# First feed-forward of a diffusion layer: tokens split 512 and 256, context high and low parts in one matmul

## What is computed

```python
def swiglu(h, w_gate, w_up, w_down):
    return (jax.nn.silu(h @ w_gate) * (h @ w_up)) @ w_down

def ffn_sublayer(t, shift, scale, gate, norm_g, w_gate, w_up, w_down):
    h = modulate(rms_norm(t, norm_g), shift, scale)
    return t + gate * (MACARON_WEIGHT * swiglu(h, w_gate, w_up, w_down))

x = ffn_sublayer(x, ml[0], ml[1], ml[2], ffn1_norm[i], ...)      # 512 tokens
ctx = ffn_sublayer(ctx, mc[0], mc[1], mc[2], ffn1_norm[i], ...)  # 256 tokens
```

## Time and profile before

| | |
|---|---|
| median of three runs | 1355.15 us (1355.12 to 1356.28) |
| span of the profiled execution | 1354.2 us |
| TensorE busy | 1333.5 us, 98% |
| VectorE busy | 865.3 us, 64% |
| ScalarE busy | 400.0 us, 30% |
| GpSimd busy | 651.0 us, 48% |

### The profile page before, as it was taken

The page is one execution under the profiler, slowest core; times in us unless marked ns, Lnnn a source line. Parts: engine busy times, 40 slices in busy tenths (PEclk is TensorE's granted clock), DMA queues, the critical chain, the costliest instruction groups (busy, mean ns, idle before and its releaser), DMA issues.

```text
span 1354.2 us, 21460 instructions
## 1 busy us (share of the span) xinstructions
PE 1333.5 (98%) x8546; PEld 1229.7 (91%) x8546; DVE 865.3 (64%) x1376; ACT 400.0 (30%) x757; POOL 651.0 (48%) x408
## 2 busy tenths in 40 slices
PE   5999999999999999999999999999999999999998
PEld 4899999999999999998888888888998999999997
DVE  5787368568556555437656649826778765555666
ACT  4320010210210110124635321222142555544455
POOL 1544444543543533532732356636467455655554
PEclk9999999999999999999999999999999999999999
DMA  9553354353444344223322479484736233344322
GB/s 357 161 148 85 121 148 120 120 157 116 126 135 139 102 126 158 62 55 109 80 62 52 126 212 259 152 266 148 229 87 199 63 94 94 107 115 114 101 72 85
DMA packets 236782, 178.18 MB, mean 132 GB/s; under 512 B 33416, under 2 KB 211852, under 8 KB 236684
## 3 DMA queue, kind: packets, MB, share of 16 engines
q1 hardware_dynamic: 216624, 145.78, 37.6%
q10 hardware_dynamic: 20060, 31.04, 7.0%
HBM read 156.93 MB, written 19.86 MB: 131 GB/s over the span
## 4 chain that ended last, share of the span: by engine, by line
PE 93%; DVE 3%; DMA 2%; SPq 1%; issue 1%; ACT 0%; DVEq 0%; ACTq 0%
PE ps L1244 47%; PE ps L1971 13%; PE ps L1566 13%; PE ps L2030 7%; DMA ada_w<-in_ada_w_dram 2%; PE ps L1255 1%; PE ps L1844 1%; DVE ada_acc L2860 1%; DVE ps L2972 1%; PE ps L2057 1%; PE ps L1881 1%; PE ps L1669 1%; PE ps L1487 1%; PE ps L1438 1%; PE ps L1706 1%
## 5 line engine op out<-in xcount | busy, mean ns | idle before, releaser
L1143 POOL TENSOR_SCALAR w_hi<-w_raw 128x1024 fp32r<-128x1024 f32 x128 | 153.4, 1198 | 527.8 <-PE ps L1244 276.0
L1146 POOL TENSOR_TENSOR w_lo<-w_raw,w_hi 128x1024 fp32r<-128x1024 f32 x128 | 325.4, 2542 | 10.7
L1244 PE MATMUL ps<-h_hi,w_lo 128*128 128x384 f32 (+2 forms) x1000 | 291.4, 351 | 0.0
L1244 PE MATMUL ps<-h_hi,w_hi 128*128 128x384 f32 (+2 forms) x1000 | 287.1, 346 | 0.0
L1244 PE MATMUL ps<-h_lo,w_hi 128*128 128x384 f32 (+2 forms) x1000 | 287.0, 346 | 0.0
L1244 PEld LDWEIGHTS ps<-h_hi,w_lo 128*128 128x128 f32 x1000 | 178.8, 188 | 14.9 <-issue 4.3
L1244 PEld LDWEIGHTS ps<-h_lo,w_hi 128*128 128x128 f32 x1000 | 180.6, 188 | 10.5
L1244 PEld LDWEIGHTS ps<-h_hi,w_hi 128*128 128x128 f32 x1000 | 180.4, 188 | 10.7
L1222 POOL TENSOR_TENSOR w_lo<-w_raw,w_hi 128x512 fp32r<-128x512 f32 x90 | 115.6, 1297 | 105.7 <-ACT w_hi L2609 104.2
L2860 DVE SCALAR_TENSOR_TENSOR ada_acc<-ada_w,cs,ada_acc 128x1024 f32<-128x1024 f32 x70 | 108.3, 1581 | 7.8 <-DMA ada_w<-in_ada_w_dram 5.5
L1971 PE MATMUL ps<-h_hi,w_hi 128*128 128x256 f32 x360 | 102.0, 283 | 0.0
(11 more groups left out here) (459 smaller groups left out, 2635.0 us busy)
## 6 DMA issues: line engine op xcount, KB each, us to landing
w_raw<-in_ffn_w_gate_dram SPq DMA_DIRECT2D x44, 512.0 KB, 5.1
w_raw<-in_ffn_w_up_dram SPq DMA_DIRECT2D x44, 512.0 KB, 4.1
w_raw<-in_ffn_w_down_dram SPq DMA_DIRECT2D x44, 512.0 KB, 4.5
ada_w<-in_ada_w_dram ACTq DMA_DIRECT2D x32, 512.0 KB, 3.9
w_raw<-in_w_in_dram SPq DMA_DIRECT2D x32, 512.0 KB, 4.3
ada_w<-in_ada_w_dram SPq DMA_DIRECT2D x30, 512.0 KB, 4.3
c_scr<-cp ACTq DMA_DIRECT2D x16, 288.0 KB, 3.8
b_scr<-bt_sb ACTq DMA_DIRECT2D x16, 256.0 KB, 3.9
```

The source lines that it names most:

```text
L1143: pool.tensor_scalar(w_hi[:, s, 0:cols], w_raw[:, s, 0:cols], 1.0, 1.0, ALU.mult, ALU.mult)\
L1146: pool.tensor_tensor(w_lo[:, s, 0:cols], w_raw[:, s, 0:cols], w_hi[:, s, 0:cols].bitcast(F32), ALU.subtract).then_inc(w_split, 1)
L1244: last = pe.matmul(mv[2], st, mv[part], start=(first and q == 0), stop=(n == len(terms) - 1 and q == 2))
```

## The change

The tokens of a gate, up or down job are now split 512 (latents) and 256 (context). The latents fill the first bank. The second bank holds two halves of 256: the high weights meet the context's high and low parts in a single matmul of 512 columns, whose moving operand has two pieces (h_pair, act_pair: the same places as before, allocated as one tile), and the low weights meet the high part in one of 256 columns that adds into the first half. A k-step has five matmuls instead of six. VectorE adds the two halves by a reduction of [128, 256, 2] to half_sum in SBUF, once behind the gate job and once behind the up job. ScalarE's silu is split in two, the second part reading half_sum and waiting for gate_summed; only it frees the pair. The product is split in two, 512 and 256. The reduction of the gate job stands first in each tile's part of VectorE's loop. The down's three adds become 256, 512 and 256. The free columns are gone in both banks of a job, so the folded sums move to the bank of the side job (in the late segment to a pair that isn't in use yet). The sums of segment 0 stay at their place, in gate 3's second bank.

```diff
-    h_hi = place("h_hi", [P, KD, NT], F32R)
-    h_lo = place("h_lo", [P, KD, NT], F32R)
+    h_pair = place("h_pair", [P, 2, KD, NT], F32R)
+    h_hi, h_lo = h_pair[:, 0, :, :], h_pair[:, 1, :, :]
...
+    act_pair = place("act_pair", [P, 2, SEG, NT], F32R)
+    act_hi, act_lo = act_pair[:, 0, :, :], act_pair[:, 1, :, :]
...
+    half_sum = place("half_sum", [P, 2, NC], F32, at=fold_at + 4 * KB)
...
+    def ctx_half(j, part):
+        return ctx_(j)[:, NC * part:NC * part + NC]
...
     def ada_sum_cols(j):
-        return lat(j)[:, ADA_COL:ADA_COL + 2 * KD]
+        return ctx_(j)[:, ADA_COL:ADA_COL + 2 * KD]
...
+                if summed:
+                    last = folded_sums(ada_sum_cols(j), summed)
                 last.then_inc(job_done, 1)
...
+                    def pair_step(j, wh, wl, hi, lo, pair, first, final, between=None):
+                        def mm(q, o, st, mv, start, stop):
+                            ins = pe.matmul(o, st, mv, start=start, stop=stop)
+                            if between and q is not None:
+                                between(q)
+                            return ins
+                        mm(None, ctx_(j), wh, pair, first, False)
+                        mm(0, ctx_half(j, 0), wl, hi[:, NL:NT], False, final)
+                        mm(None, lat(j), wl, hi[:, 0:NL], first, False)
+                        mm(1, lat(j), wh, lo[:, 0:NL], False, False)
+                        return mm(2, lat(j), wh, hi[:, 0:NL], False, final)
...
-                            for q in range(2):
-                                pe.matmul((lat, ctx_)[q](js.gu(v))[:, 0:384], st[:, k, :],
-                                          h_hi[:, k, 384 * q:384 * q + 384], start=(k == 0 and r == 0), stop=False)
+                            for o, c in ((lat(js.gu(v)), slice(0, NL)), (ctx_half(js.gu(v), 0), slice(NL, NT))):
+                                pe.matmul(o, st[:, k, :], h_hi[:, k, c], start=(k == 0 and r == 0), stop=False)
...
+                        if two:
+                            last = pair_step(j, wh[:, k, c], wl[:, k, c], act_hi[:, k, :], act_lo[:, k, :], act_pair[:, :, k, NL:NT],
+                                             k == 0, k == tiles - 1)
...
                         if n == NT:
-                            dst, src = dst.rearrange("p (b c) -> p b c", b=2), both(jg, 384)
-                        act.wait_ge(job_done, (jg + 1) + i * part.jseg)
+                            act.activation(dst[:, 0:NL], src, ACT.Silu)
+                            act.wait_ge(gate_summed, i * SEG + (part.segs * SEG + f + 1))
+                            dst, src = dst[:, NL:NT], half_sum[:, 0, :]
                         act.activation(dst, src, ACT.Silu).then_inc(slot_read[jg % 4], 1)
...
                     for f_ in range(tiles):
                         jg, ju = js.gu(2 * f_), js.gu(2 * f_ + 1)
+                        if n == NT:
+                            done(jg)
+                            sum_halves(jg, 0).then_inc(gate_summed, 1)
                         if part.side:
...
+                            up = tokens(ju)
+                            link(sum_halves(ju, 1))
...
+                        elif n == NT:
+                            STT(up[:, 0:NL], up[:, 0:NL], 0.5, sl[:, 0:NL], ALU.mult, ALU.mult)
+                            STT(up[:, NL:NT], half_sum[:, 1, :], 0.5, sl[:, NL:NT], ALU.mult, ALU.mult).then_inc(gu_ok, 1)
...
+                            half = STT(x[:, k, c], ctx_half(j, 0), mod[:, g, 1:2], x[:, k, c], ALU.mult, ALU.add)
+                            own[0] += 1
+                            half.then_inc(dve_own, 1)
+                            STT(x[:, k, 0:NL], lat(j), mod[:, g, 0:1], x[:, k, 0:NL], ALU.mult, ALU.add)
+                            dve.wait_ge(dve_own, own[0])
+                            ins = STT(x[:, k, c], ctx_half(j, 1), mod[:, g, 1:2], x[:, k, c], ALU.mult, ALU.add)
...
+            def sum_halves(j, n):
+                return dve.tensor_reduce(half_sum[:, n, :], ctx_(j).rearrange("p (h c) -> p c h", h=2), AX.X, ALU.add)
```

More of the change, by code:

```diff
@@ L1330, in _, with s5_side @@
             keep_busy(5)
-            def s5_side(i, v, j):
+            def s5_side(i, v, j, summed):
                 h = v // 2
@@ L1479, in slot_free, with pair_job @@
                         pe.wait_ge(slot_read[j % 4], j // 4 + i * (part.jseg // 4))
+                    def pair_step(j, wh, wl, hi, lo, pair, first, final, between=None):
[9 more added lines that the diff above has]
+                        return mm(2, lat(j), wh, hi[:, 0:NL], False, final)
+                    def pair_job(j, wh, wl, between=None):
+                        for k in range(KD):
+                            last = pair_step(j, wh[:, k, :], wl[:, k, :], h_hi[:, k, :], h_lo[:, k, :], h_pair[:, :, k, NL:NT], k == 0, k == KD - 1,
+                                             (lambda r: between(k, r)) if between else None)
+                        return last
                     joint = 2 if two and part.segs + i == 0 else 0
@@ L1492, in joint_lo @@
                         wh = wv((u0 + v) % 4, KD, P)[0]
-                        for q in range(2):
-                            last = pe.matmul((lat, ctx_)[q](js.gu(v))[:, 0:384], wh[:, k, :],
-                                             h_lo[:, k, 384 * q:384 * q + 384], start=False, stop=(k == KD - 1))
+                        pe.matmul(lat(js.gu(v)), wh[:, k, :], h_lo[:, k, 0:NL], start=False, stop=(k == KD - 1))
+                        last = pe.matmul(ctx_half(js.gu(v), 1), wh[:, k, :], h_lo[:, k, NL:NT], start=False, stop=(k == KD - 1))
                         if k == KD - 1:
@@ L1540, in sums_between @@
                                     ada_sum(ada_ctx_cols(js.gu(v - 1)), ADA_START, n)
-                            last = split_mm(terms, sums_between)
+                            last = pair_job(j, wh, wl, sums_between)
+                        elif two:
+                            if part.late and v == 3:
+                                pe.wait_ge(tail_cols_read, 1)
+                            last = pair_job(j, wh, wl)
+                            if part.late and v == 1:
+                                slot_free(js.gu(3))
+                                last = folded_sums(ada_sum_cols(js.gu(3)), g)
                         else:
                             last = split_mm(terms)
-                        if two and nth and g and v == 1:
-                            last = folded_sums(ada_sum_cols(j), g)
                         if not two and nth == 0 and v == 2 * tiles - 1:
@@ L1563, in down_step @@
                         c = slice(P * q, P * q + P)
-                        for r, (st, mv) in enumerate(((wl, act_hi), (wh, act_lo), (wh, act_hi))):
-                            for bank, cols in down_banks(j, two):
-                                last = pe.matmul(bank, st[:, k, c], mv[:, k, cols], start=(k == 0 and r == 0),
+                        if two:
+                            last = pair_step(j, wh[:, k, c], wl[:, k, c], act_hi[:, k, :], act_lo[:, k, :], act_pair[:, :, k, NL:NT],
+                                             k == 0, k == tiles - 1)
+                        else:
+                            for r, (st, mv) in enumerate(((wl, act_hi), (wh, act_lo), (wh, act_hi))):
+                                last = pe.matmul(lat(j), st[:, k, c], mv[:, k, 0:NL], start=(k == 0 and r == 0),
                                                  stop=(k == tiles - 1 and r == 2))
@@ L3183, in seg @@
                         if n == NT:
[L3184 to L3190 removed]
+                            up = tokens(ju)
+                            link(sum_halves(ju, 1))
+                        if q == 0 and nth == 0 and f_ == tiles - 1:
+                            ada_bias(ada_ctx_cols(jg), ada_summed(nth))
+                        if part.late and f_ == 0:
+                            sums_bias(ada_sum_cols(js.gu(3)), ada_summed(nth)).then_inc(tail_cols_read, 1)
                         if q and nth == 0 and f_ == tiles - 1:
@@ L3226, in seg @@
                             done(j)
+                            if f_ == 0 and ada_summed(nth):
+                                sums_bias(ada_sum_cols(j), ada_summed(nth))
                             s5_lags(i, f_, j, lambda: read(j))
```

47 lines of the change are left out of this document (16 added, 31 removed).

## The result

The changed kernel takes 1390.15 us (median of 4 runs, 1389.17 to 1391.74); the kernel before, run beside it, 1355.13 us (1354.66 to 1356.28). The ratio is 1.0256 with a 95% interval of 1.0242 to 1.0271.

The account below looks back on a forecast made before the run. It took TensorE, busy 98% of the span, as the bound. Terms of 8.8 + 1.7 + 1.1 + 0.3 - 1.7 = +10.2 us on the 1354.2 us span, with the median 0.95 above, gave 1365.3 us, range 1358 to 1372.

Parts of the forecast that it names:

- What bounds the kernel: Whole kernel: TensorE, busy 98% of the span, sets the time; other engines count only where TensorE waits for them.
- Matmuls, -1.7 us: Gate, up and down steps: five matmuls instead of six gain 1.7 us, between 6.6 gained and 5.0 lost.
- The joint start, +0.24: Joint start: same number of matmuls, now 512 and 256 wide; 12 steps at 20 ns lose 0.24 us.
- VectorE's work in full segments, nothing: Segments with S5 work: added reductions and split products are covered by VectorE's idle time and cost nothing.
- the cover of 3.99 us: VectorE's idle time before a segment's last tile, taken to hide its added work in segments with S5 work.
- a hole at other jobs: Stated sign of being wrong: TensorE gaps at other jobs' starts mean VectorE's added work isn't covered in S5 segments.
- The stall of segment 0, +8.8 (5.5 to 13.2): Last up job of segment 0: TensorE's first modulation sum waits 8.8 us for gate 3's reduction, queued behind VectorE's older work.
- The choice between the ends: Segment 0 stall: multiply-adds taken as done at 106.7, roots at 110.0, between ends of 106.7 and 114.4.
- The clock, +1.7 (0 to 3.4): Behind segment 0's stall: a mixed full and half clock loses 1.7 us, as behind an earlier, shorter idle time.
- Rival 2: Stall occurs, but the clock stays up and weight-load savings come in full: 1358.8 us, chance 0.15.
- The end of the last segment, +1.1: Last segment's end: the VectorE and ScalarE chain TensorE awaits grows from 2.2 to 3.3 us, 1.1 longer (0.9 to 1.3).
- The third down of segment 0, +0.05: Segment 0's third down waits for a product taking some 2.1 us against a cover of 2.08: 0.05 us.

Follow-up runs that it names:

- the sum in the bank: Changed kernel with the up job's two halves added in their own bank, and one product over 768 columns: 1375.61 us, ratio 1.0149.
- the run with the sums behind the job: Changed kernel with segment 0's sixteen column sums in one row behind the fourth up job's last matmul, waits unmoved: 1385.01 us, ratio 1.0219.
- both edits: Changed kernel with segment 0's roots behind the fourth gate's reduction and the up halves added in their own bank: 1366.55 us, ratio 1.0077.
- the wait alone: Kernel before the change, with ScalarE's silu of segment 0's fourth gate made to wait until VectorE has done the roots: 1371.72 us, ratio 1.0115.

## Why the prediction was right and wrong, step by step

It forecast 1365.3 us with a range of 1358 to 1372. The sign and most places were right, the size was not: 25 us are missing. Two steps failed above all: VectorE's work in the full segments, put at nothing, cost 9.3 us, and the half clock behind the hole, put at 1.7, cost 9.4.

- **What bounds the kernel** held: what was lost lies in holes of TensorE and in its clock, and the segments without a hole (3 and 4) kept their time.
- **Matmuls, -1.7 us.** (Its own figures, 336 x 6.7 - 160 x 3, give 1.8.) Measured 0: 105.08 against 105.12 us a segment, and a gate or up job of segment 3 took 8.34 us against 8.36. The two effects of the estimate are both there, 11 ns a step for the instruction saved (charged 13.3) and 11 for the uneven widths; the second was charged too low (6.7).
- **The joint start, +0.24:** it ended 0.1 us later.
- **VectorE's work in full segments, nothing.** Wrong: 7.6 us of holes in segments 1 and 2, and 1.7 us of clock. Two sizes failed. The 256-wide product was put at 0.40 us, one of the "estimates from the earlier trace rows"; it takes 2.54 in the median, since it reads two tiles of SBUF while GpSimd subtracts. The row that shows such a collision was in hand: 2.43 us for an operation of 0.22 beside GpSimd was used for the old operations and not asked of the new one. And the cover of 3.99 us was read in segment 3, where VectorE has seven multiply-adds of the modulation; segments 1 and 2 have fourteen each, and before the change the last tile of segment 2 had 1.73 us of idle time where segment 3 had 3.99. Timeline of VectorE of the kernel before:

```profile
321.28 0.97 DVE L3203 SCALAR_TENSOR_TENSOR ps<-ps,silu 128x768 f32<-128x768 f32 x1 [1.73 <-PE ps L1244]
```

  The blocked product was the decisive one of the two: without it the same cover was enough (the sum in the bank). The text had said what a hole at other jobs would mean; that is what came.
- **The stall of segment 0, +8.8 (5.5 to 13.2).** Place, releaser and queue were right: the reduction stands behind the multiply-adds and the roots. It is 12.35 us in this profile, because the block slipped nearly whole. Timeline of VectorE of the changed kernel (answers to the earlier trace rows):

```profile
101.36 4.65 DVE L2891 SCALAR_TENSOR_TENSOR ada_acc<-ada_w,cs,ada_acc 128x1024 f32<-128x1024 f32 x2 [0.23 <-DVE act_pair L3242]
...
106.08 2.21 DVE L2778 TENSOR_TENSOR powers<-s5t 128x64 f32<-128x64 f32 x1
...
109.32 2.37 DVE L2780 TENSOR_SCALAR s5t<-powers 128x64 f32<-128x64 f32 x1
...
114.07 0.69 DVE L3314 TENSOR_REDUCE half_sum<-ps 128x256 f32<-128x512 f32 x1
```

  The choice between the ends was wrong. The roots were put at 3.3 us on the ground that GpSimd would have ended at 106.7; but its work moved too and ended at 111.64, the roots met it again (2.21, 1.08 and 2.37 us) and took 8.1 us. The start of 101.36 is the "about 101" of the prediction, but by luck. In the run with the sums behind the job, where VectorE has the same work in the same order, the last multiply-adds start at 98.25. The difference begins with two S5 operations that took 1.10 and 2.46 us beside GpSimd in the changed kernel, and 0.22 and 0.23 in that run. Timeline of VectorE, first of the changed kernel, then of that run:

```profile
67.32 1.10 DVE L2767 TENSOR_TENSOR s5t<-s5t 128x64 f32<-128x64 f32 x1
68.46 2.46 DVE L2768 TENSOR_TENSOR s5t<-s5t 128x64 f32<-128x64 f32 x1
```

```profile
67.00 0.23 DVE L2767 TENSOR_TENSOR s5t<-s5t 128x64 f32<-128x64 f32 x1
...
98.25 4.71 DVE L2890 SCALAR_TENSOR_TENSOR ada_acc<-ada_w,cs,ada_acc 128x1024 f32<-128x1024 f32 x2 [0.23 <-DVE act_pair L3241]
```

  The same two operations were slow in the profile with both edits (1.08 and 2.47 us), and there the hole was 3.81 us, not 1.70. In the run with the sums behind the job the multiply-adds ended at 102.96 and the hole was 9.57 us, with the sum in the bank 9.32. That is within a microsecond of the 8.8 forecast, but by two errors that nearly cancel: the multiply-adds ended 3.3 to 3.7 us earlier than 106.7, and the roots took 8.1 us and not 3.3.
- **The clock, +1.7 (0 to 3.4).** Measured 9.4 us behind this hole, 7.7 more than forecast, and two shorter stretches of half clock elsewhere (224 and 637 us). A hole of 2.4 us followed by 3.4 us of half clock was carried over to a longer hole as the same loss. Behind this hole stand the one-column sums, and the clock came back only behind the last of them: 20.2 us of half clock here, 20.9 in the wait alone, 5.4 where the sums stood elsewhere. Rival 2 had the clock stay up; no case had it stay down.
- **The end of the last segment, +1.1.** The hole grew by 2.54, and 3.4 us of half clock follow it. Its cause, again, is the product; with the product in the bank the growth is 1.61 - 0.47 = 1.14, the term as worked out. Timeline of the changed kernel (answers to the earlier trace rows):

```profile
632.47 2.36 POOL L1151 TENSOR_TENSOR w_lo<-w_raw,w_hi 128x1024 fp32r<-128x1024 f32 x1
632.61 2.50 DVE L3230 SCALAR_TENSOR_TENSOR ps<-half_sum,silu 128x256 f32<-128x256 f32 x1
```

- **The third down of segment 0, +0.05:** 0.85, by the same product.

Added up, in us: 9.3 in the full segments, 7.7 for the half clock, 3.6 for the stall, 1.7 for the matmuls, 1.4 and 1.7 at the end of the last segment (hole and clock) and 0.8 at the third down are some 26, where 25.6 are missing between the spans.

So the steps that failed are these. The product's new operand was not priced against GpSimd's work, 0.40 us for 2.54, and the cover was read where VectorE has less to do; the full segments lost 9.3 us where nothing was charged. And the loss of clock behind a short hole was carried over to this one, 1.7 us for 9.4. The term for the tail came out as worked out once the block is taken away (1.14 for 1.1); that of the stall came near only by errors that cancel.

## What to carry to other kernels

When a change swaps an operand's place (a bank for a tile of SBUF), price the operation by its new operands and by what the other engines do at that very moment; two engines released by the end of the same job can collide again and again, here with the full length of a subtraction in 15 cases of 21. A hole of TensorE must be priced with the work behind it: here the clock came back only behind the last one-column matmul, which cost some 9 us more for holes of 7.0 and 12.35. And fewer instructions for the same columns are worth only what their new widths leave of it.

## What the runs showed of the hardware that was not expected

- Behind a hole of 3.8 to 12.4 us the granted clock stayed at half for 19 to 21 us of a busy TensorE when one-column matmuls stood between the whole ones (four kernels), for 5.4 us behind a hole of 9.6 when they didn't (one kernel). Behind a hole of 1.7 us at the same place it stayed up (one kernel), and behind the holes of 2.47 to 2.50 us in segments 1 and 2 it fell for 3.4 us in six cases of eight (four kernels). Directly behind a row of such matmuls of 3.6 us the clock fell for 3.4 us without any idle time before it (two kernels).
- A VectorE product of 256 columns with two SBUF inputs took 0.42 us or up to 2.56, by whether and how long before GpSimd had begun a subtraction; the 512-wide product with one input in PSUM took 0.70 right beside it.
- The same 2304 columns a step took as long in five matmuls of 512 and 256 as in six of 384, 11 ns more in six of 512 and 256, and 32 ns more in nine of 256.
